# A hybrid decoder trunk on one core: where the modulation's row products stand in a level of the delta rule

## What is computed

```
c_act = silu(c)                          # (1, 2048)
mod   = c_act @ ada_w[i] + ada_b[i]      # (2048, 12288), float32
sh1, sc1, g1, sh2, sc2, g2 = split(mod, 6)
```

```
lower = where(strict, (k_beta @ k.T) * decay, 0)
T     = inverse(eye + lower)
u, w  = T @ v_beta, T @ (k_beta * exp(g))
per chunk: v_new = u - w @ S;  o = q_decay @ S + intra @ v_new;  S = S * g_last + k_tail.T @ v_new
```

## Time and profile before

| | |
|---|---|
| runs | median 2753.8 us (2752.7 to 2761.28, 3 runs) |
| profiled execution | 2753.74 us, its span 2752.1 us |
| TensorE busy | 2562.4 us, 93% of the span |
| VectorE, ScalarE busy | 1950.6 us (71%), 1222.8 us (44%) |
| chain that ended last | TensorE 83%, VectorE 10%, DMA 3%, ScalarE 2%, issue 2% |
| mean granted clock of TensorE | 0.959 |
| loads of `ada_w` slots from SP | 80 of 512 KB, 4.7 us from issue to landing (median) |

### The profile page before, as it was taken

How to read it: one execution, slowest core, us unless ns; L and a number is a source line. 1 busy time by engine, 2 the same in 40 slices (tenths; PEclk the granted TensorE clock), 3 DMA queues, 4 the chain that set the end, 5 groups by cost and what they waited for, 6 DMA issues and landing times.

```text
span 2752.1 us, 42348 instructions
## 1 busy us (share of the span) xinstructions
PE 2562.4 (93%) x16852; PEld 2287.2 (83%) x16852; DVE 1950.6 (71%) x2406; ACT 1222.8 (44%) x1619; POOL 198.8 (7%) x226
## 2 busy tenths in 40 slices
PE   1499999999889999999999899998899999999997
PEld 1488888777878899889988799998878998899887
DVE  8878997554487777777778898569887655555556
ACT  1255666444464433443343454553454434443444
POOL 0012332000000000000001011000000000000000
PEclk8589999999999999999999899999999999999998
DMA  9864443655448888888888499456588656555652
GB/s 374 288 246 153 170 147 129 230 184 182 144 153 300 276 272 283 274 285 279 278 274 286 153 343 342 164 175 218 181 275 276 217 194 191 190 184 187 196 183 77
DMA packets 272988, 616.04 MB, mean 224 GB/s; under 512 B 23211, under 2 KB 23746, under 8 KB 272578
## 3 DMA queue, kind: packets, MB, share of 16 engines
q1 hardware_dynamic: 240020, 488.00, 52.1%
q0 software_dynamic: 32640, 125.84, 13.1%
q10 hardware_dynamic: 174, 0.04, 0.0%
HBM read 611.73 MB, written 2.10 MB: 223 GB/s over the span
## 4 chain that ended last, share of the span: by engine, by line
PE 83%; DVE 10%; DMA 3%; ACT 2%; issue 2%; SPq 0%; DVEq 0%; POOL 0%; POOLq 0%; ACTq 0%
PE groups L2533 12%; PE groups L2535 11%; PE groups L2537 11%; PE groups L2525 11%; PE groups L2529 11%; PE groups L2527 11%; DMA ada_units<-in_ada_w_dram 3%; DVE ada_acc L2025 2%; PE pc L2704 2%; PE pm L873 1%; DVE ada_acc_other L2350 1%; PE pb L2694 1%; DVE w_lo L2043 1%; DVE ada_acc L2350 1%; PE groups L1124 1%
## 5 line engine op out<-in xcount | busy, mean ns | idle before, releaser
L1742 ACT ACTIVATE w_hi<-w_raw 128x1024 fp32r<-128x1024 f32 x776 | 817.2, 1059 | 1127.8 <-PE groups L2529 543.5
L2043 DVE TENSOR_TENSOR w_lo<-w_raw,w_hi 128x1024 fp32r<-128x1024 f32 x747 | 905.2, 1223 | 527.4 <-ACT w_hi L1742 523.7
L2525 PE MATMUL groups<-w_hi,act_hi 128*128 128x512 f32 x1408 | 553.3, 393 | 20.2 <-DVE act_lo L2177 20.2
L2529 PE MATMUL groups<-w_lo,act_hi 128*128 128x512 f32 x1408 | 549.7, 390 | 0.0
L2527 PE MATMUL groups<-w_hi,act_lo 128*128 128x512 f32 x1408 | 549.7, 390 | 0.0
L2533 PE MATMUL groups<-act_hi,w_hi 128*128 128x256 f32 x1776 | 510.2, 287 | 33.0 <-DVE act_lo L2177 14.0
L2535 PE MATMUL groups<-act_lo,w_hi 128*128 128x256 f32 x1776 | 501.8, 283 | 0.0
L2537 PE MATMUL groups<-act_hi,w_lo 128*128 128x256 f32 x1776 | 501.5, 282 | 0.0
L2533 PE MATMUL groups<-hid_hi,w_hi 128*128 128x256 f32 x1392 | 390.5, 281 | 0.0
L2535 PE MATMUL groups<-hid_lo,w_hi 128*128 128x256 f32 x1392 | 388.8, 279 | 0.0
L2537 PE MATMUL groups<-hid_hi,w_lo 128*128 128x256 f32 x1392 | 388.7, 279 | 0.0
(11 more groups left out here) (434 smaller groups left out, 2403.1 us busy)
## 6 DMA issues: line engine op xcount, KB each, us to landing
ada_units<-in_ada_w_dram POOLq DMA_DIRECT2D x120, 1024.0 KB, 6.7
w_raw<-in_ffn_w_gate_dram SPq DMA_DIRECT2D x88, 1024.0 KB, 5.3
w_raw<-in_ffn_w_up_dram SPq DMA_DIRECT2D x88, 1024.0 KB, 5.2
w_raw<-in_ffn_w_down_dram SPq DMA_DIRECT2D x88, 1024.0 KB, 5.2
w_raw<-in_cd_w_in_dram SPq DMA_DIRECT2D x48, 1024.0 KB, 5.6
w_raw<-in_ab_w_in_dram SPq DMA_DIRECT2D x40, 1024.0 KB, 5.2
ada_units<-in_ada_w_dram SPq DMA_DIRECT2D x80, 512.0 KB, 4.7
w_raw<-in_ab_w_out_dram SPq DMA_DIRECT2D x16, 1024.0 KB, 7.1
```

Source lines behind the costliest of these rows:

```text
L1742: act.activation(whi[:, half, k], raw[:, slot, k], ACT.Copy).then_inc(hi_done, 1)
L2043: dve.tensor_tensor(wlo[:, half, k], raw[:, slot, k], whi[:, half, k].bitcast(F32), ALU.subtract).then_inc(lo_done, 1)
L2525: pe.matmul(dst, hi[:, k, rows], whi[:, j % 2, kk], start=(k == 0), stop=False, skip_group_check=True)
L2529: last = pe.matmul(dst, hi[:, k, rows], wlo[:, j % 2, kk], start=False, stop=(k == UK * p["units"] - 1), skip_group_check=True)
```

## The change

In every level `ada_rows` moves from behind `add_up` to ahead of `side`, that is between `turn_half` (and `ada_sum`, where there is one) and the side product. In level 0, which has no sum product, `power_up` and `gram_q` now come first, then the row products, then the side product. The programs of the other engines and of the queues stay word for word.

```
                         turn_half(i, k - 1)
                     for pair in ada_due(i, k):
                         ada_sum(pair)
-                    if side_at(i, k) >= 0:
-                        side(out0b, side_at(i, k))
                     if k == 0:
                         power_up(i, k)
                         gram_q(i)
+                    ada_rows(pe, 8 * EARLY_PAIRS + len(LEAD_ROWS) + LEVELS * i + k)
+                    if side_at(i, k) >= 0:
+                        side(out0b, side_at(i, k))
                     if k == 1 and nxt:
                         row_g(i + 1)
...
                     if k:
                         add_up(i, k)
-                    ada_rows(pe, 8 * EARLY_PAIRS + len(LEAD_ROWS) + LEVELS * i + k)
                     if k == 5 and nxt:
                         norm_k(i + 1)
```

## The result

The changed kernel took 2774.87 us (median of five runs, 2765.72 to 2781.2) against 2756.4 us for the kernel before in the same sitting: a ratio of 1.0061, 95% interval 1.0042 to 1.0080. It is slower, and lies above 2771 us, the upper end of the predicted range. Two more sets gave smaller ratios, 1.0035 (1.0019 to 1.0051) and 1.0049 (1.0030 to 1.0067). All 21 runs of the changed kernel have a median of 2770.3 us; the kernel before, in 25 to 35 runs of each later sitting, has 2756.5 to 2758.8.

A forecast was written before the change was run, and what follows sets the result against it. TensorE was taken to bound the kernel, with nothing to fill in the rounds. Terms 4.2 + 0 + 2.3 + 0.6 + 0.8 + 2.1 + 1.6 = 11.6 us on 2753.7 gave 2765.3 us, range 2758 to 2771.

The forecast's parts named there:

- item 3: Levels (0,4), (1,5), (2,6): row products wait for VectorE's take, no longer hidden by the side product; 2.3 us in all.
- 1. The merge: Between sum product and next power product: VectorE's merge loses the cover of the row products; 4.2 us.
- 2. Round 0, level 1: Row products fill a 1.45 us hole, but level 2 at half clock loses it again; 0, between -0.5 and 0.5 us.
- 4. ScalarE: Level (1,4): output copy waits for a later out_intra, delaying ada_sum of (1,5); 0.6 us, between 0 and 0.9.
- item 7: TensorE's clock, around (0,4) and (3,2): one more stretch at half clock, 1.6 us, between none and three stretches.
- 5. Level 0: Round 1: the power product waits for VectorE's lower, no longer hidden by the side product; 0.8 us.
- 6. The transfer: Level (3,2): row products wanted earlier wait for late loads queued behind a weight unit; 2.1 us.
- rival C: More half clock from merge holes and longer ada_sum holes: three more stretches cost 4.8, total 16.4 us, 2770.1; chance 0.12.
- Rival A: Transfer of (3,2) hidden and clock holds: only 7.9 us more, 2761.7, no measurable change; chance 0.24.
- B: Round 0's slow stretch regains full clock sooner: up to 5.0 us back, 6.6 more, 2760.4, not slower; chance 0.12.
- the signs: Expected in the rounds: named waits for merge, take (longest in (2,6)), load in (3,2) and lower; rounds 8 to 14 us longer.

The follow-up runs named there:

- the takes alone: Kernel before with row products ahead of the side product only in levels (0,4), (1,5) and (2,6); 2757.62 us, ratio 1.0004.
- only the stepped levels: Kernel before with row products ahead of the side product only in eleven levels where a step of the round before follows the sum product; 2762.56 us, ratio 1.0016.

## Why the prediction was right or wrong

**Direction and mechanism** were right: nothing to fill, covers lost, slower. The sum without the clock was 10.0 us, and the traces show about 10 (192 to 193.5 against 182 to 183 at full clock). That the two agree so well is in part luck: the merge cost more than forecast, and the takes and the transfer less. The rows below are those of (2,6) in the changed kernel, for item 3:

```profile
652.71 3.58 PE L1272 MATMUL pm<-ident,ada_acc 128*128 128x2 f32 x16 [1.18 <-ACT ada_acc L879]
...
656.54 1.94 PE L873 MATMUL pm<-ada_units,c_act 128*32 128x512 f32 x8 [0.26 <-DVE mod L1015]
```

By item:

1. The merge: 4.2 predicted, about 5.5 measured. Bare it cost 0.69, as said; under a step 0.26 on average and not 0.13 (0.26 x 12 = 3.1), since the first weight load of the power product is bare as well; the extra 0.3 for (2,3) did not come. Level 5 of round 3 cost 0.96, not 0.9. The Trainium skill's rule on weight loads that run ahead ("TensorE: Matmul & The Clock Gate", Part 2) does not help here: in the row of 528.09 the load starts with its matmul, after the wait.
2. Round 0, level 1: 0 predicted, between -0.9 and +0.8 measured, by the clock.
3. The take: 0.4 each predicted and 0.26 measured in (0,4) and (1,5); for (2,6) with level 0 behind it 1.5 predicted, 1.08 measured, and not by the path described. The wait for the take was 0.26 us in the changed kernel, where 1.15 was predicted and 0.99 measured with the takes alone: the thin matmuls ahead took 3.58 us, partly at half clock, and 2.50 in the kernel before, and most of the wait lay under them. A wait of 0.72 us for ScalarE's copy ahead of gram came in its place.
4. ScalarE: 0.6 predicted, 0.43 measured (1.39 against 0.96), and item 7 hangs on it.
5. Level 0: 0.8 predicted, 1.05 measured in the whole change, 0.8 alone. By the rule of item 1 it should have had the restart too: 0.76 to the end of lower and 0.15 are 0.9.
6. The transfer: 2.1 predicted. (3,2) grew by 3.47, of which 0.25 belong to the merge and at most 1.7 to the clock, which leaves 1.5 or somewhat more. With its share of items 1 and 7 the level was forecast to grow by 3.8. Its loads did keep their place: they went out 3.2 us behind the power product of (3,1) before and 3.3 after. They landed 0.4 us later each; the next slot's loads, now earlier, follow at once, which may be why, but no run tests it.

**The step that failed is item 7.** It priced one stretch of half clock, 1.6 us, at (3,2). That one came, in size and place. But the places that fell already did not stay as they were: with their fixed costs (1,5) took 0.5, 3.6 and 2.2 us more in three traces, (0,4) 0.9, 3.7 and 0.9. In the stage the share of half clock was 20.6 us on average and 17.0 before, so the term should have been near 4, with a scatter from about 0 to 8 between executions. Some of it comes back behind the stage: from the power product of (3,6) to the start of the products behind the rounds' last long wait (3.58 us) it is 27.2 us in both traces of the kernel before, and 24.5, 24.5 and 27.2 in the changed one.

In its place the runs showed two things. First, (1,5) took 11.5 to 11.6 us in the four traces where the wait ahead of ada_sum is 0.96 us (the kernel before twice, the takes alone, level 0 alone), and 12.1 to 15.2 in the six where it is 1.39 (the changed kernel three times 12.08, 15.15 and 13.71, the others 13.63 to 13.70). Only 0.4 of that is the wait itself, so the clock does more there behind the longer wait; that the wait is the cause is likely but was not tested by itself. Second, (0,4) went from 9.8 to 11.4 us with the order and the wait of the kernel before, in the run with only the stepped levels: part of the term is scatter that any execution can have. The bare merges are not where the clock fell: levels (1,1) to (1,4) and (0,3) agree within 0.04 us in the three traces. That part of rival C, a fall in more places, did not come; the time of all 21 runs, 2770.3 us, equals C's 2770.1, but as a difference from the kernel before (11.5 to 13.8 us) it lies between the forecast's 11.6 and C's 16.4.

**The base** failed as well. 2753.8 us was the median of three runs of a kernel that scatters over 13 us; 25 to 35 runs gave 2756.5 to 2758.8. The forecast of +11.6 us on that base would have been 2768 to 2770, and the 21 runs have 2770.3. The first five runs of the changed kernel, on which it was measured, lay 4.6 us above that. So of the 9.6 us between the forecast and the measured 2774.87, 2.6 are the base of the same sitting (2756.4 against 2753.8) and 4.6 the chance of five runs; the remaining 2.4 are what item 7 was short of in the stage. A range built from costs in a trace needs the scatter of the execution as a term of its own, and this one had none.

Rival A did not come (the transfer was late), nor B: (0,1) and (0,2) together took 22.7 to 23.5 us, 22.6 and 23.6 before. Of the signs, the merges, the takes, lower and the load were named as said (TensorE waited 1.8 us for the first of the two loads, and its weight loads 3.1 for both), but the wait for the take in (2,6) was no longer than the others, and the stage was 14.2 us longer on average, just outside the 8 to 14.

What stays open is why the clock falls for longer in one run than in the next, and what level 0 alone costs in its usual execution: it measured 4 us, and the one trace is of a quick run and shows one.

## What to carry to other kernels

In a loop with two latencies, filler belongs under the one whose own cover is short: add up, for each wait, the work behind it until the next dependent instruction, before moving any. A block that is moved takes its own waits along, and here the load of (3,2) was nearly harmless only where it was wanted last. If a kernel's runs scatter by as much as the effect, read the effect as distances between like instructions of several traces, times the clock there, and take the base from many runs.

## What the runs showed of the hardware

A weight load behind a semaphore wait was not hidden here: the power product took 0.94 us to the turn after a wait and 0.84 without. Two executions of one program differed by 2.7 us in one level of 10.7 while the granted clock was 0.84 in one and 0.62 in the other. And half clock followed 0.96 us of idle time with 1.95 us of thin matmuls (two columns each) behind it, although TensorE counts as busy in the second; with 1.5 us of real work in place of the idle time three levels were 8.5 us shorter, though 3.7 of it came back in (0,5) and (2,0).
